# One product per head for the softmax denominators, with one more VectorE add per head

## The reference, cut to what matters

```python
s = jnp.einsum('bkgqd,bskd->bkgqs', qi, k, preferred_element_type=F32) * scale
p = jax.nn.softmax(s, axis=-1).astype(v.dtype)
return jnp.einsum('bkgqs,bskd->bkgqd', p, v)
```

## Time and profile before

| | |
|---|---|
| median of 3 runs | 1456.26 us (1449.04 to 1456.75) |
| profiled execution | 1449.79 us |
| its span, first to last instruction | 1448.0 us |
| PE busy | 1378.6 us, 95% |
| DVE busy | 921.9 us, 64% |
| ACT busy | 586.9 us, 41% |
| POOL busy | 552.3 us, 38% |
| mean granted TensorE clock | 0.985 |

### The profile page before, as it was taken

How to read it: one execution, slowest core, us unless ns; L and a number is a source line. 1 busy time by engine, 2 the same in 40 slices (tenths; PEclk the granted TensorE clock), 3 DMA queues, 4 the chain that set the end, 5 groups by cost and what they waited for, 6 DMA issues and landing times. The chain is left out here.

```text
span 1448.0 us, 15401 instructions
## 1 busy us (share of the span) xinstructions
PE 1378.6 (95%) x5940; PEld 1034.7 (71%) x5940; DVE 921.9 (64%) x992; ACT 586.9 (41%) x864; POOL 552.3 (38%) x287
## 2 busy tenths in 40 slices
PE   7999989998999999999999998998989999999998
PEld 5587654377788888788876785444768888887886
DVE  6776876547777787611286778665478878784213
ACT  6222455534544444422252225454354343433223
POOL 3222333036443434444552314320464444444443
PEclk9999999999999999999999999999999999999999
DMA  7212301022333333233341222100323333323332
GB/s 268 73 29 66 82 12 33 1 58 67 94 88 102 88 101 89 86 100 95 99 136 53 58 55 50 30 15 1 88 61 99 88 102 88 101 84 95 95 94 85
DMA packets 205538, 112.53 MB, mean 78 GB/s; under 512 B 15303, under 2 KB 202425, under 8 KB 204570
## 3 DMA queue, kind: packets, MB, share of 16 engines
q1 hardware_dynamic: 205466, 111.54, 26.4%
HBM read 105.63 MB, written 2.10 MB: 74 GB/s over the span
## 5 line engine op out<-in xcount | busy, mean ns | idle before, releaser
L509 POOL TENSOR_TENSOR wl<-raw,wh 128x1024 fp32r<-128x1024 f32 x176 | 430.9, 2449 | 699.3 <-ACT wh L588 699.2
L588 ACT ACTIVATE wh<-raw 128x1024 fp32r<-128x1024 f32 x176 | 186.4, 1059 | 562.1 <-PE ps L1103 528.9
L1101 PE MATMUL ps<-gh,wh 128*128 128x512 f32 (+1 forms) x864 | 346.4, 401 | 4.4 <-POOL wl L509 4.4
L1102 PE MATMUL ps<-gl,wh 128*128 128x512 f32 (+1 forms) x864 | 341.5, 395 | 0.0
L1103 PE MATMUL ps<-gh,wl 128*128 128x512 f32 (+1 forms) x864 | 341.5, 395 | 0.0
L1101 PEld LDWEIGHTS ps<-gh,wh 128*128 128x128 f32 (+1 forms) x864 | 161.9, 187 | 48.4 <-issue 7.8
L1102 PEld LDWEIGHTS ps<-gl,wh 128*128 128x128 f32 (+1 forms) x864 | 161.8, 187 | 40.6 <-issue 1.9
L1103 PEld LDWEIGHTS ps<-gh,wl 128*128 128x128 f32 (+1 forms) x864 | 161.9, 187 | 39.4
L1541 DVE TENSOR_TENSOR acc<-acc,sq 128x512 f32<-128x512 f32 x24 | 60.6, 2523 | 191.1 <-ACT sq L632 190.9
L1971 DVE SCALAR_TENSOR_TENSOR cv<-pad,pm,cv 128x512 f32<-128x512 f32 x88 | 130.6, 1484 | 77.7 <-ACT cv L960 77.7
L1101 PE MATMUL ps<-fh,wh 128*128 128x512 f32 x308 | 121.7, 395 | 0.7 <-POOL wl L509 0.7
(11 more groups left out here) (274 smaller groups left out, 2221.0 us busy)
## 6 DMA issues: line engine op xcount, KB each, us to landing
raw<-w_up SPq DMA_DIRECT2D x88, 512.0 KB, 3.8
raw<-w_down SPq DMA_DIRECT2D x32, 512.0 KB, 3.8
raw<-w_in SPq DMA_DIRECT2D x30, 512.0 KB, 4.0
raw<-w_out SPq DMA_DIRECT2D x16, 512.0 KB, 4.2
raw<-w_down SPq DMA_DIRECT2D x16, 384.0 KB, 3.4
xio<-x SPq DMA_DIRECT2D x4, 512.0 KB, 4.2
win<-c_win SPq DMA_DIRECT2D x2, 1024.0 KB, 5.7
TF<-c_tf SPq DMA_DIRECT2D x2, 1024.0 KB, 8.9
```

Of the source, the lines that this page charges most:

```text
L509: nc.gpsimd.tensor_tensor(l, raw[:, slot, :], h.bitcast(F32), ALU.subtract).then_inc(S["lo_ready"], 1)
L588: A(xh[:] if third(lay, n) else wh[:, slot, :], raw[:, slot, :], ACT.Copy).then_inc(S["hi_ready"], 1)
L1101: mm(ps[0:cols, bank, :], w_hi, x_hi, start=start and k == 0, stop=False)
L1102: mm(ps[0:cols, bank, :], w_hi, x_lo, start=False, stop=False)
```

## The change

`row_sums` now adds once more: after `tsum[:, h % 2, 0:2, :]` is there, DVE waits for its own result and adds the part 1 to the part 0 (128x512), and only then signals `summed`. `denominators` multiplies the ones by part 0 alone, so that a pair takes two products instead of four. Nothing else is changed: the 24 calls of `row_sums` (12 heads, 2 layers) stay where they were in DVE's order, and the 12 calls of `denominators` in PE's.

```diff
                     free7("den", p)
                     pe.wait_ge(S["summed"], lay * HEADS + 2 * p + 2)
-                    for part in range(2):
-                        for half in range(2):
-                            ins = mm(ps[half * GD:(half + 1) * GD, 7, :], ones[:, 0:GD], tsum[:, half, part, :],
-                                     start=(part == 0), stop=(part == 1))
+                    for half in range(2):
+                        ins = mm(ps[half * GD:(half + 1) * GD, 7, :], ones[:, 0:GD], tsum[:, half, 0, :], start=True, stop=True)
                     ins.then_inc(S["den_mm"], 1)
...
                     pT = probT[h % 4]
-                    tt(tsum[:, h % 2, :, :], pT[:, 0:2, :], pT[:, 2:4, :], ALU.add).then_inc(S["summed"], 1)
+                    V.do(tt(tsum[:, h % 2, :, :], pT[:, 0:2, :], pT[:, 2:4, :], ALU.add))
+                    V.join()
+                    tt(tsum[:, h % 2, 0, :], tsum[:, h % 2, 0, :], tsum[:, h % 2, 1, :], ALU.add).then_inc(S["summed"], 1)
```

## The result

The changed kernel took 1459.59 us (median of 12 runs) against 1452.53 of the kernel before, run with it: a ratio of 1.0049, 95% interval 1.0034 to 1.0063, that is +7.1 us (4.9 to 9.2). In a second set on another occasion it was 1.0043 (1.0025 to 1.0061). The forecast was +8.6 us. As a time it named 1464.9, 5.3 us too much: 3.7 of them because it was put on 1456.26, the median of three runs, where twelve runs give 1452.53. One of those twelve took 4746 us and is left out of the ratio.

A forecast was written before the change was run, and what follows sets the result against it. PE bounds outside the attention stage; inside, PE and DVE take turns being late. Waiting less saved work, 2 x 3.44 = +6.9 us, plus +1.7 for clock made +8.6 on 1456.26: 1464.9 us, range 1452 to 1474.

The forecast's parts named there:

- What is removed: In denominators, half of the products go: 0.86 us saved per call, 12 calls, 10.3 us of PE work.
- Rival 5: In denominators, the halves stop overlapping, a call gives 0.43 us, not 0.86: +4.3 on the forecast, 1469; chance 0.07.
- What is added: In row_sums, 24 SBUF adds of 128x512 on DVE, each delaying what follows by 0.83 us: 20 us.
- peaks(4, 2): Behind row_sums(1), the bare add delays PE by +0.83 us; PE's stall there becomes 2.2 us.
- The flip at q_lo(5): At row_sums(2), tsum is issued ahead of POOL's q_lo(5): peaks(5, 0) shifts +1.78 us, or 1.41 if POOL comes first.
- q_lo(7): Row_sums(4) meets POOL's q_lo(7) as before, its add then waits for q_lo; group(0) comes at +1.88 us.
- The held add of row_sums(5): POOL's wl holds the add, 2.7 us long: 1.63 us more, shift +3.51 at peaks(8, 2); lower end 0.
- The saved 0.86 of the pairs 2 and 3: After peaks(8, 2), PE's shift falls to +2.65 us at denominators(2) and from +2.8 to +1.94 at denominators(3).
- The clock: After new PE stalls, half clock costs up to 1.7 us a stretch; two stretches, half of each swallowed: +1.7 us.
- The plain walk: Whole stage: the add costs 0.83 us wherever it stands, POOL never matters; +1.0 in all, 1457.3 us; chance 0.27.
- PE as the bound: Whole stage: PE alone decides, all adds lie in DVE's idle time; -10.3 us, 1446.0; chance 0.04.
- Rival 4: The clock falls after most new stalls, six more stretches at 1.7 us: +17, 1473 us; chance 0.12.

The follow-up runs named there:

- e4_qlo_first: The changed kernel with POOL's q_lo(h+1) done ahead of shift(h) for h = 2 to 6: ratio 0.9997, -0.4 us against the kernel before.

## Why the prediction was right

It forecast +8.6 us and +7.1 was measured. The cause that it named, added waiting on VectorE that is more than the work saved on PE, is what the runs show. That the number is so near is in part luck: it had +6.9 for waiting less work and +1.7 for the clock, and in the profiled stages they were +2.5 and +5.7. Point by point:

- **What is removed.** Right. One `denominators` now takes 1.00 us where the clock is full (247.78 to the next matmul at 248.78, shown above) instead of 1.86. Rival 5, that the halves stop overlapping, fell with it.
- **What is added.** The mechanism was right, the size too large. From the timeline of DVE after, row_sums(1) with nothing of POOL beside it:

```profile
204.99 1.21 DVE L1765 TENSOR_TENSOR tsum<-probT 128x1024 f32<-128x1024 f32 x1
206.24 0.69 DVE L1767 TENSOR_TENSOR tsum<-tsum 128x512 f32<-128x512 f32 x1
206.85 0.68 DVE L1747 TENSOR_TENSOR ckl<-ckv,ckh 128x512 fp32r<-128x512 f32 x1
```

  The next instruction starts 1.86 us after tsum's start, 1.14 before: the add costs 0.72, not 0.83. The gap behind tsum is 0.04, where the pair of the earlier trace rows had 0.15. POOL ran beside the second one of that pair, which lasted 0.91, but that isn't the reason: in e4_qlo_first, with POOL elsewhere, it lasts 0.69 and starts 0.83 after the first all the same. Why this pair has the longer gap no run shows. The kernel before had a nearer pair in the rotations, at 213.19 and 213.90, a step of 0.71. The Trainium skill ("VectorE: DVE Perf Modes", section on the DRAIN) has nothing extra for the semaphore; the trace has 0.11 us over the 0.61 of an unjoined step, halfway between the page and my term. In the last chain of the stage this term stands twice, and with 0.72 its +0.67 becomes the 0.44 that were measured (from 4.31 to 4.75).
- **peaks(4, 2)** came +0.74 (0.83 forecast), stall 2.12 against the 2.2 named.
- **The flip at q_lo(5)** did not happen in the profiled execution: the clock was at half there, tsum came 0.26 us after q_lo, and DVE waited instead. The timelines of DVE and POOL:

```profile
212.93 2.11 DVE L1765 TENSOR_TENSOR tsum<-uc 128x1024 f32<-128x1024 f32 x1 [1.51 <-PE ps L1399]
```

```profile
212.67 1.28 POOL L537 TENSOR_TENSOR q2c<-qf,q2c 64x512 fp32r<-64x512 f32 x1
```

  That the shift there is +1.81, where the flip would have made +1.78, is luck: from `peaks(4, 2)` to the product PE took 3.54 us (208.19 to 211.73) instead of 2.07 (206.77 to 208.84) because of the half clock, and that stood in for the flip. In the four stages of the changed kernel's two traces q_lo(5) came first each time, by 0.26 to 0.86 us. At full clock the flip did happen, in the run with half the products and in layer 0 of the one with wl moved: 0.91 and 0.89 us later, where 0.95 was the price.
- **q_lo(7)** was missed. The walk has row_sums(4) meet it "as before". But denominators(1) is 0.86 shorter too, and by the same subtraction tsum comes at 226.62 - 0.86 = 225.76, ahead of q_lo(7) at 225.92. The timelines of POOL and DVE in the kernel before:

```profile
225.92 1.28 POOL L537 TENSOR_TENSOR q<-qf,q 64x512 fp32r<-64x512 f32 x1
```

```profile
226.62 1.67 DVE L1767 TENSOR_TENSOR tsum<-probT 128x1024 f32<-128x1024 f32 x1 [1.95 <-PE ps L1400]
```

  and of DVE and POOL in the changed one:

```profile
228.85 1.23 DVE L1765 TENSOR_TENSOR tsum<-probT 128x1024 f32<-128x1024 f32 x1 [1.10 <-PE ps L1399]
```

```profile
229.00 2.20 POOL L537 TENSOR_TENSOR q<-qf,q 64x512 fp32r<-64x512 f32 x1
```

  PE then stalls 1.72 us before `peaks(7, 0)`, in all four stages of the changed kernel. With the adds alone, where the product isn't shorter, that stall doesn't exist. So group(0) came late by way of POOL (+2.54 instead of +1.88), and not by the sum of squares: in this stage its own stall, 1.13 before, is gone.
- **The held add of row_sums(5)** was right: 2.7 was named, 2.77 measured, and the copy behind it then stopped the bank-7 product for 1.20 us. The step from `group(0)` to `peaks(8, 2)` is 2.65 longer than before, of which 1.63 were named. The rest lies in the stretch at half clock at 232.1: up to the next `peaks` at 237.03 PE took 3.93 us, against 2.89 before.
- **The saved 0.86 of the pairs 2 and 3** came as forecast: from +5.19 to +4.31 at `group(1)`, -0.88, where the walk had -0.74.
- **The clock** was under-priced. I took two stretches, half swallowed, 1.7 us. The stages had seven stretches with half clock in them in each of the changed kernel's two traces, against three before. The stall before `peaks(4, 2)` was followed by one four times of four (before, never in two), and that before `yl` three times of four (before, never). By the table above they cost 5.7 us more. The runs say the same: the spans times the missing part of the clock give 1457 x 0.0155 = 22.6 us and 1457 x 0.0136 = 19.8 us in the changed kernel's two sets, and 1450 x 0.0112 = 16.2 us before: 4 to 6 us more, not all of it on the path. That the sum still came out near is because the waiting was over-priced: +2.5 instead of +6.9, two errors of opposite sign, of about 4 us each. They are not independent, since PE at half clock is late by itself and then waits less, as at q_lo(5).
- **The chances.** The measured +7.1 is at the bound of 7.3 between "no change that can be told" and "slower", where 0.46 and 0.50 had been set. The plain walk (+1.0, chance 0.27) is refuted by the adds alone (+13.5 against +7), PE as the bound (0.04) by half the products alone. Rival 4 (the clock, 0.12) was half right: its sign was more than four new stretches, and there were four, but its +17 us is far outside the interval.

## What to carry to other kernels

Before an instruction is added to an engine, look not only at what waits for it but at which other engine's instruction runs beside it: an add with both inputs in SBUF, in front of which POOL's 2.4 us operation was already queued, took 2.77 us. The same add done by POOL while VectorE reads PSUM held up one product, by 1.5 us, until it was placed better, though it is dearer by itself (1.27 against 0.69). A saving ahead of a wait on a third engine can change who is first and come out as a loss; take the order on that engine first, at every place where the saving moves something, and only then count the saving. Split a result into waiting, work and clock before you explain it: moving q_lo was meant to take away stalls, gave 7 us, and left PE's waiting as it was.

## What was not expected of the hardware

Between two executions of one kernel the granted clock differs (0.980 to 0.994 over the runs of the kernel before), and with it which of two engines is first at a shared resource: the 12 runs with wl moved spread over 12.5 us, the six of the fastest kernel over 6.9. An edit that removed 1.20 us of stall and 2.08 us of a held add in each layer was not visible in the median of 12 runs. Moving q_lo gave 7 us although the stalls that it removed (1.27 and 1.7 us in each layer) came back before other instructions. And the length of a stall alone doesn't tell what the clock does: 2.12 us before `peaks(4, 2)` was followed by half clock in all four stages of the changed kernel, and 3.16 us at the same place, with q_lo first, by the full clock in both layers (1.00 from 919.30 to 922.70). What decides it these runs don't show.
